# Building each chunk's 64x64 inverse before the state needs it, in a chunked RWKV-7 recurrence

## What is computed

```python
def step(S, inp):
    r_t, w_t, k_t, v_t, kk_t, a_t = inp
    sa = jnp.einsum('bhvk,bhk->bhv', S, -kk_t)
    S = (S * w_t[:, :, None, :]
         + sa[..., None] * (kk_t * a_t)[:, :, None, :]
         + v_t[..., None] * k_t[:, :, None, :])
    y = jnp.einsum('bhvk,bhk->bhv', S, r_t)
    return S, y
```

## Time and profile before

| what | value |
|---|---|
| median of three runs | 772.66 us |
| the profiled execution | 773.59 us, of which its span is 771.9 us |
| PE busy | 740.1 us, 96% of the span |
| DVE busy | 428.4 us, 56% |
| ACT busy | 229.5 us, 30% |
| 16 DMA engines, 262 to 500 us (the chunks) | 21% busy |
| PE busy, 650 to 700 us (experts) | 50.00 of 50 us |

### The profile page before, as it was taken

The page is one execution under the profiler, slowest core; times in us unless marked ns, Lnnn a source line. Parts: engine busy times, 40 slices in busy tenths (PEclk is TensorE's granted clock), DMA queues, the critical chain, the costliest instruction groups (busy, mean ns, idle before and its releaser), DMA issues.

```text
span 771.9 us, 19753 instructions
## 1 busy us (share of the span) xinstructions
PE 740.1 (96%) x8328; PEld 527.0 (68%) x8328; DVE 428.4 (56%) x862; ACT 229.5 (30%) x543; POOL 45.3 (6%) x53
## 2 busy tenths in 40 slices
PE   7999999999999999999999999999999699999995
PEld 5887787787778777778878878778887533333331
DVE  5956667788787675756565564465223442212146
ACT  5122222254523333333323344310031501111145
POOL 0000000000000000010000000000000112221221
PEclk9999999999999999999999999999999689999998
DMA  9562432531221101121442102183934789999965
GB/s 324 205 207 85 155 126 72 209 114 56 73 91 56 56 30 58 58 59 44 148 119 59 57 30 84 44 332 122 409 125 167 250 349 397 392 402 390 377 211 220
DMA packets 38135, 130.43 MB, mean 169 GB/s; under 512 B 6267, under 2 KB 16763, under 8 KB 33184
## 3 DMA queue, kind: packets, MB, share of 16 engines
q1 hardware_dynamic: 32544, 115.07, 40.1%
q0 software_dynamic: 5504, 14.10, 6.2%
HBM read 111.13 MB, written 18.66 MB: 168 GB/s over the span
## 4 chain that ended last, share of the span: by engine, by line
PE 86%; DVE 5%; DMA 4%; issue 2%; ACT 1%; POOL 0%; SPq 0%; POOLq 0%; DVEq 0%; ACTq 0%
PE psum L1457 23%; PE psum L1812 11%; PE psum L1438 11%; PE psum L2784 9%; PE psum L2818 4%; PE psum L1415 4%; DVE arena L2184 3%; PE psum L1402 2%; PE psum L1390 2%; PE psum L1664 1%; PE psum L2764 1%; PE psum L1678 1%; PE psum L1580 1%; PE psum L1675 1%; DMA u_rows<-arena 1%
## 5 line engine op out<-in xcount | busy, mean ns | idle before, releaser
L2184 DVE TENSOR_TENSOR arena<-arena 128x268 f32<-128x268 f32 (+13 forms) x322 | 176.5, 548 | 47.6 <-ACT arena L1911 28.3
L1457 PE MATMUL psum<-arena 128*128 128x268 f32 x784 | 188.4, 392 | 0.0
L1457 PEld LDWEIGHTS psum<-arena 128*128 128x128 f32 x784 | 145.6, 190 | 33.0 <-issue 6.7
L1911 ACT ACTIVATE arena<-psum 128x268 f32<-128x268 f32 (+7 forms) x207 | 83.0, 410 | 258.9 <-PE psum L1457 138.6
L1911 ACT ACTIVATE arena<-arena 64x256 f32<-64x256 f32 (+11 forms) x173 | 69.0, 430 | 104.1 <-PE psum L1824 57.7
L1438 PE MATMUL psum<-arena 128*128 128x260 f32 x392 | 96.9, 392 | 0.8 <-DVE arena L2184 0.6
L2184 DVE TENSOR_TENSOR arena<-psum,arena 128x256 f32<-128x256 f32 (+7 forms) x151 | 60.4, 405 | 55.5 <-PE psum L1678 12.4
L1812 PE MATMUL psum<-arena 128*128 128x260 f32 x384 | 88.3, 385 | 1.5 <-DVE arena L2184 0.8
L2784 PE MATMUL psum<-arena 128*32 128x512 f32 (+1 forms) x640 | 86.7, 604 | 0.5 <-DVE arena L2949 0.3
L1438 PEld LDWEIGHTS psum<-arena 128*128 128x128 f32 x392 | 70.9, 189 | 17.3 <-issue 5.4
L1812 PEld LDWEIGHTS psum<-arena 128*128 128x128 f32 x384 | 71.3, 190 | 15.4 <-DVE arena L2187 2.1
(11 more groups left out here) (233 smaller groups left out, 669.0 us busy)
## 6 DMA issues: line engine op xcount, KB each, us to landing
arena<-in_w_gu SPq DMA_DIRECT2D x16, 2048.0 KB, 19.7
arena<-in_w_in SPq DMA_DIRECT2D x45, 512.0 KB, 4.2
arena<-in_w_dn SPq DMA_DIRECT2D x16, 1024.0 KB, 17.2
arena<-in_w_out SPq DMA_DIRECT2D x2, 2048.0 KB, 14.9
arena<-in_x SPq DMA_DIRECT2D x8, 268.0 KB, 6.0
arena<-arena SPq DMA_DIRECT2D x16, 134.0 KB, 4.4
arena<-in_x SPq DMA_DIRECT2D x1, 2144.0 KB, 14.5
arena<-arena SPq DMA_DIRECT2D x4, 520.0 KB, 6.5
```

The lines of the kernel that those rows point to most:

```text
L1457: last = mm(ps, w[:, k, :], x[:, k, :], start=(k == 0 and i in (0, 1, 3)), stop=(k == KD // 2 - 1), skip_group_check=i not in (0, 1, 3))
L1911: run(nc.scalar.activation(out, in_, fn, **kw), s)
L2184: run(v.tensor_tensor(out, a, b, op), s)
```

## The change

The inverse of a whole 64x64 chunk has the two 32x32 inverses on its diagonal and, below them, (second inverse) x (block below) x (first inverse). The change builds that last block too:

- `wk_t` of level 16 makes 8 products more, for the first half's other form, and DVE adds 256 columns instead of 128.
- A new step `wk_x` of level `H` = 32: 8 products of 32x32 (`below` by the first inverse), copied by DVE into `tp`. It stands where `wk_sa` stood, in the second burst.
- A new step `wk_u`: 8 products of 32x32 with the second inverse, copied by ACT (two copies) into the new tile `inv`. It stands first in the third burst, where `wk_y` stood.
- A new step `wk_w`: four ACT copies of the two diagonal inverses into `inv`, among the pieces after the second burst. Two DVE memsets in `st0` clear the rest of `inv` once.
- `wk_sa` is now 8 products of 64x64 by 64 columns with `inv`, in the fourth burst, where `wk_sb` stood. `wk_y` and `wk_sb` are gone, with DVE's sum; ACT's two copies of 64 rows replace four of 32.
- `xl` and the PSUM columns of `wk_x` and `wk_t` are doubled (by c % 2), and several waits are looser: `wk_a` and `wk_k` no longer wait for `s_y1`, and `s_ab` counts two steps a chunk.
- The four `tg` sums: one moves to c = -2 (after burst 4), the others stand after bursts 1, 2 and 4 of c = -1.

`TAKES` and the number of bursts stay. The 16-token chunk keeps its old way.

```diff
@@ bursts
-                of(c + 1, ("wk_t", 4)) + of(c, ("wk_sa",)),
-                of(c, ("wk_y",)) + of(c + 2, ("wk_d",)) + of(c + 1, ("wk_x", 8)),
-                of(c + 1, ("wk_t", 8)) + of(c + 2, ("wk_x", 2)) + of(c, ("wk_sb",)) + of(c + 1, ("wk_a",)),
+                of(c + 1, ("wk_t", 4)) + of(c, ("wk_x", H)),
+                of(c, ("wk_u",)) + of(c + 2, ("wk_d",)) + of(c + 1, ("wk_x", 8)),
+                of(c + 1, ("wk_t", 8)) + of(c + 2, ("wk_x", 2)) + of(c, ("wk_sa",)) + of(c + 1, ("wk_a",)),
@@ between
-        between = [prep(c + 2, ("wk_p", 4), ("wk_p", 5)), so[0:1],
-                   ([("wk_e", c + 3)] if c + 3 < len(CHUNKS) else []) + so[1:2],
+        between = [prep(c + 2, ("wk_p", 4), ("wk_p", 5)), of(c, ("wk_w",)) + so[0:1], of(c + 3, ("wk_e",)) + so[1:2],
-        if c == -1:
-            for i in range(1, 5):
-                between[i].append(("tg", i - 1))
+        for i, x in {-2: ((4, 0),), -1: ((1, 1), (2, 2), (4, 3))}.get(c, ()):
+            between[i].append(("tg", x))
@@ PE, wk_x
+                        if b == H:
+                            if d == 0:
+                                last = mm(psum[64 * s + H:64 * s + 64, 2304 + H * p:2304 + H * p + H], below[g, p, :],
+                                          tp[c % 3][g, 0, p, :], start=True, stop=True)
+                            continue
@@ PE, wk_t
-                    if 2 * b < n:
-                        for p, s, d, g, rd in tiles_of(c):
+                    for p, s, d, g, rd in tiles_of(c):
+                        if 2 * b < n or CHUNKS[c][1] == C and d == 0:
@@ PE, new
+                elif kind == "wk_u":
+                    c = step[1]
+                    pe.wait_ge(s_xl, X_N[(c, H)])
+                    for p, s, d, g, rd in tiles_of(c):
+                        if d == 1:
+                            last = mm(psum[64 * s:64 * s + H, 3840 + H * p:3840 + H * p + H], tp[c % 3][g, 0, p, :],
+                                      tp[c % 3][g, 1, p, :], start=True, stop=True)
@@ PE, wk_sa
+                    if CHUNKS[c][1] == C:
+                        pe.wait_ge(s_y1, 6 * (c + 1))
+                        for p in range(NP):
+                            for s in range(2):
+                                _, _, full, _ = wk(c, s)
+                                last = mm(psum[full, 3328 + 64 * p:3328 + 64 * p + 64], inv[full, p, :], rr[full, p, :],
+                                          start=True, stop=True)
@@ ACT, new
+                elif kind == "wk_w":
+                    c = step[1]
+                    act.wait_ge(s_tt, T_N[(c, 16)])
+                    if c:
+                        act.wait_ge(s_psa, 2 * c)
+                    for p, s, d, g, rd in tiles_of(c):
+                        if p == 0:
+                            f(inv[g, :, rd], tp[c % 3][g, 1], s=s_y1)
+                elif kind == "wk_u":
+                    c = step[1]
+                    act.wait_ge(s_py, c + 1)
+                    for s in range(2):
+                        f(inv[half(s, H), :, H:C], psum[half(s, H), 3840:3968].rearrange("t (p k) -> t p k", p=NP), s=s_y1)
@@ DVE
+                    if b == H:
+                        run(v.tensor_copy(tp[c % 3][:, 0], psum[:, 2304:2432].rearrange("t (p k) -> t p k", p=NP)), s_xl)
+                        continue
-                elif kind == "wk_y":
...
-                    tt(rr, psum[:, 1536:1792].rearrange("t (p k) -> t p k", p=NP), rr, ALU.add, s=s_y1)
```

More of the change, by code:

```diff
@@ L357, in of @@
         return [(x[0], c, *x[1:]) for x in steps if 0 <= c < len(CHUNKS)
-                and (x[0] not in ("wk_x", "wk_t") or x[1] < CHUNKS[c][1]) and (x[0] not in ("wk_y", "wk_sb") or CHUNKS[c][1] > H)]
+                and (x[0] not in ("wk_x", "wk_t") or x[1] < CHUNKS[c][1])
+                and (x[0] not in ("wk_u", "wk_w", "wk_b") or CHUNKS[c][1] > H)]
     def bursts(c):
         return [of(c, ("wk_t", 16)) + of(c + 1, ("wk_x", 4)) + of(c, ("wk_r",)) + of(c + 1, ("wk_k",)),
-                of(c + 1, ("wk_t", 4)) + of(c, ("wk_sa",)),
-                of(c, ("wk_y",)) + of(c + 2, ("wk_d",)) + of(c + 1, ("wk_x", 8)),
-                of(c + 1, ("wk_t", 8)) + of(c + 2, ("wk_x", 2)) + of(c, ("wk_sb",)) + of(c + 1, ("wk_a",)),
+                of(c + 1, ("wk_t", 4)) + of(c, ("wk_x", H)),
+                of(c, ("wk_u",)) + of(c + 2, ("wk_d",)) + of(c + 1, ("wk_x", 8)),
+                of(c + 1, ("wk_t", 8)) + of(c + 2, ("wk_x", 2)) + of(c, ("wk_sa",)) + of(c + 1, ("wk_a",)),
                 of(c + 2, ("wk_t", 2)) + of(c + 1, ("wk_x", 16)) + of(c, ("wk_s",))]
@@ L382, in order @@
     bonus += [("j_bon", p, hf) for p in range(NP) for hf in range(2)]
-    s += take(6)
+    s += take(TAKES_FIRST)
     for c in range(-2, len(CHUNKS) - 1):
@@ L563, in hybrid_step @@
         below = at(NP * H, NP, H, start=CON["reset"][0])
+        inv = at(NP * C, NP, C, start=CON["reset"][0] + NP * H)
+        xl = [xl, at(NP * H, NP, H, start=CON["reset"][0] + NP * (H + C))]
+        assert NP * (2 * H + C) <= TP
         w_ba = [at(2048, KD // 2, NP, P, start=x) for x in (base - 4 * T - RH * T, u_end)]
@@ L832, in hybrid_step, with burst_of, first_and_last @@
         X_N, T_N = count_of("wk_x"), count_of("wk_t")
+        def burst_of(step):
+            n0 = n1 = STEPS.index(step)
+            while STEPS[n0 - 1][0].startswith("wk_"):
+                n0 -= 1
+            while STEPS[n1 + 1][0].startswith("wk_"):
+                n1 += 1
+            return STEPS[n0:n1 + 1]
+        def first_and_last(step, count):
+            x = [count[s[1:]] for s in burst_of(step) if s[0] == step[0]]
+            return x[0] - 1, x[-1]
+        X_RUN = {x: first_and_last(("wk_x", *x), X_N) for x in X_N}
+        T_RUN = {x: first_and_last(("wk_t", *x), T_N) for x in T_N}
         PAB = {s: n + 1 for n, s in enumerate([s for s in STEPS if s[0] in ("wk_d", "wk_a")])}
@@ L2064, in _ @@
                         act.wait_ge(s_act, own[0])
-                elif kind == "wk_b" and CHUNKS[step[1]][1] > H:
+                elif kind == "wk_b":
                     c = step[1]
@@ L2353, in _ @@
                 elif kind == "st0":
+                    for i in range(2):
+                        run(v.memset(inv[64 * i + H:64 * i + C, :, 0:H], 0.0))
                     job_done(dve, ("j_w", len(PAIRS) - 1, SEVEN - 1))
@@ L2403, in _ @@
                     if i == 4 and c >= 3:
+                        dve.wait_ge(s_kq, 2 * RH + 4 * (c - 3) + 2)
+                    if i == 5 and c >= 3:
                         dve.wait_ge(s_ps, 2 * c - 4)
@@ L2443, in _ @@
                     _, w, _, _ = wk(c, 0)
[L2444 to L2447 removed]
+                    dve.wait_ge(s_pr, T_RUN[(c, b)][1])
+                    n, o = min(w, H), 2560 + 256 * (c % 2)
+                    f0 = 0 if 2 * b < n or w == C else 1
+                    ps = psum[:, o:o + 256].rearrange("t (a p k) -> t a p k", a=2, p=NP)
                     tt(tp[c % 3][:, f0:2, :, 0:n], ps[:, f0:2, :, 0:n], tp[c % 3][:, f0:2, :, 0:n], ALU.add, s=s_tt)
[L2449 to L2453 removed]
                 elif kind == "wk_s":
```

101 lines of the change are left out of this document (38 added, 63 removed).

## The result

The change takes **776.33 us** (median of 7 runs, 775.03 to 782.59) against 772.47 of the kernel before, run beside it on the same chip (771.59 to 776.41): a ratio of 1.0049, with an interval of 1.0025 to 1.0073. The forecast was 769.8 with a range up to 773.0, so it missed on the slow side by 6.5 us. The profiled execution of the change took 775.36 us.

What follows compares the result with a forecast made beforehand. PE, busy 96% of the span, was taken as the bound. Savings of 1.8 + 1.1 = 2.9 us took the profiled 773.59 to 770.7, or 769.8 us on the medians' scale; range 767.6 to 773.0.

Steps and rivals of the forecast that it cites:

- term 1: PE's products in a full chunk: 1.69 us becomes 1.46, saving 0.23 a chunk, 1.8 us over eight.
- the sentence that priced the added instructions at nothing: PE's instruction stream: 256 more instructions in all, 1.5%, about one more queue packet, with no time charged.
- term 2: PE's 1.1 us wait for DVE at chunk 0's level-16 `wk_t` goes, as one `tg` sum moves earlier.
- What bounds the kernel: In the chunks PE, busy 233.4 of 238 us, sets the pace; shortening the state's chain alone gains nothing.
- a little for the change to another shape: Allowance on each new group of 8 products by 32 columns: 0.29 us taken against a row of 0.27.
- My row of 0.27 us: PE's step of 16 products by 32 columns over four strips, taken as nearest to the new 8-product groups.
- The 60-cycle rule: Skill's rule that a matmul costs some 60 cycles whatever its width, so halved groups would cost as much as old.
- width does not count: Rival: 8 products on two strips are paced by weight loads, 0.57 us each, giving 776.6 us; chance 0.03.
- What costs nothing: DVE's and ACT's changed work, memsets, looser waits and added instructions cost no time; ACT some 9 us against 156 idle.
- The sign that I had named for it: In the profile after, PE's pauses without a releaser adding up to more than before would show the forecast wrong.
- pauses of the instruction stream: Rival: PE pauses 1.08 us in each other chunk's grown first burst, costing 7.6 us, giving 777.4; chance 0.06.

Runs made afterwards that it cites:

- e1: The change once more with no edit, for a second profile and comparison; 778.34 us, 1.0052 of the kernel before.
- e4: The change with `wk_u` behind `wk_d` in the third burst, so a step of its own tile shape follows it; 776.33 us, 1.0037.
- e2: The kernel before with only the new places of the four `tg` sums; 771.95 us, 0.9984 of the kernel before.
- e13: e2's version with eight level-16 `wk_t` products repeated per full chunk, 32 instructions more; 779.13 us, 1.0061 of the kernel before.
- e14: The change without the eight products it adds to level-16 `wk_t` per full chunk, 32 instructions fewer; 772.18 us, 0.9984 of the kernel before.
- e3: The change with the four `tg` sums in their old places; 778.09 us, 1.0067 of the kernel before.
- e8: e2's version with 12 small idle products (48 instructions) ahead of PE's first step; 777.57 us, 1.0055 of the kernel before.
- e12: e2's version with 56 small idle products (224 instructions) ahead of PE's first step; 777.69 us, 1.0054 of the kernel before.
- e6: The change with 48 small idle products (192 instructions) ahead of PE's first step; 780.26 us, 1.0092 of the kernel before.
- e9: The change with 64 small idle products (256 instructions, one whole block) ahead of PE's first step; 780.71 us, 1.0096 of the kernel before.

## Why the prediction was wrong

Two steps failed: the size of term 1, and the sentence that priced the added instructions at nothing. The loss adds up as -1.2 (term 2) + 0.4 (products: the first three rows of the table, 45.07 - 44.69) + some 3.5 (blocks) = 2.7 us. By the ratios it is 3.8 in the first comparison and 4.0 in e1, and the intervals reach down to 1.9 and 2.6.

- **What bounds the kernel**: right. PE does, and the shorter chain of the state brought nothing by itself, since nobody waited for it.
- **Term 1, the products of a full chunk**: mis-sized, +0.4 us instead of -1.8. The eight products in `wk_t`, with the same shape behind them, take the 0.29 that I took (20.74 - 18.39 over eight chunks). The level-32 `wk_x` and `wk_u` take 0.37, `wk_sa` 0.61 for 0.59, and the `wk_x` ahead of `wk_sa` 0.10 more than before. Over eight chunks this is 8 x (0.08 + 0.08 + 0.02 + 0.10) = 2.2 us. I had set aside "a little for the change to another shape"; it is 0.10 us (0.38 against 0.28 for the same `wk_x`, and e4's burst). My row of 0.27 us had the same shape behind it, while each of the three old steps had another shape or filler behind it, so their 0.56 to 0.57 had the price in it: I compared rows of two kinds. The Trainium skill (TensorEngine Tiling (Array Packing), section Key Properties) says that changing the tiling mode drains TensorE; the rows agree, and I had not applied it. The 60-cycle rule of the Trainium skill (the same page, section Performance Considerations), my rival "width does not count", did not decide: 0.37 is not 0.57.
- **Term 2**: right, in place and size. e2 shows it alone.
- **What costs nothing**: right for DVE, ACT, memsets and looser waits. The last sentence is the step that failed most: I counted 256 more instructions as one more packet and priced it at nothing. They are 32 a chunk, and they move every block of 256 behind them. e13 and e14 show that this costs some 3.5 us here. The sign that I had named for it is there: between 260 and 500 us the pauses of 0.3 us or more without a releaser come to 2.0 us, and to 4.1 in e1, against 1.6 before.
- **The rivals**: "pauses of the instruction stream" is what happened. That its price (777.4) lay near the time is luck, as it took off a gain of 1.8 us from term 1 that did not come; and I gave it 0.06 and had the wrong mechanism. I looked for a pause in each chunk, from a first burst that had grown. There are two to four in the profiled runs of the change (the first two, e3, e4), in whichever burst a block begins with its packet late. And I read the two pauses of the kernel before as its normal state. Of the four places tried for that order (in e2's version), the one that it has is the best.

The profiled runs alone would not have shown the size: between the two of the first comparison the pauses of 0.3 us or more differ by only 0.5 us, between e1's and that of before by 2.6. The same kernel has other pauses in one trace than in the next (2.0 us in the change, 4.1 in e1), and its time spreads over 7 us; that the one makes the other is likely, but not shown, as only the profiled runs show their pauses.

## What to carry to other kernels

Where PE is the bound and works through hundreds of small products without a break, count instructions as well as time: a packet of instructions has to arrive every 256, and an edit anywhere ahead moves all the places where that can go wrong. Before an edit of under 1% is judged, run it at two or three alignments (idle products ahead of the first step do it); the spread here, 4 to 6 us, was larger than anything the edit did by its own work. And price a small step by a row with the same kind of step behind it: the shape that follows is in its time.

## What was unexpected of the hardware

- A packet's request is late without any other transfer in its way. In the change it starts 4.0 us after the block's beginning at 431.28, with no DMA packet on the core from 431.3 to 435.2. At the same block it was 3.6 to 4.1 us late in e1, e3 and e4, while the middle half of the packets in the chunks start 0.7 to 1.7 us behind their block's beginning. What decides this stays open; with it stays open which alignment will be good.
- After a long pause TensorE's clock can fall. In e1 PE idled 1.77 us up to 291.82. Then the stretches 291.8 to 292.5, 292.5 to 295.9 and 295.9 to 299.0 us read (granted clock ahead of the last two numbers):

```profile
291.80:292.50 0.70, 0.68 (x11) 0.61 (x12) 0.54 (x4) 0.18 (x1) 0.00 (x0) 1.00 0.04 12
292.50:295.90 3.40, 3.40 (x14) 2.88 (x12) 0.86 (x4) 1.99 (x5) 0.00 (x0) 0.50 0.02 5
295.90:299.00 3.10, 3.10 (x90) 2.54 (x89) 1.71 (x4) 1.50 (x5) 0.00 (x0) 1.00 0.17 28
```

The granted clock is 0.50, the lower level of 1.2 GHz, for 3.4 us, and the filler's records start 0.43 us apart in it instead of 0.22. Against the median of the six traces this costs e1 another 1.7 us, as much as the pause itself. e8 and e12 show the same at pauses of 2.18 and 1.94 us; in e6 the clock stayed at 1.00 behind one of 1.94. At the pause of 1.5 us ahead of the chunks that all 18 traces have, it fell in two (e8, e9).
